# Gate rows and self-attention weights by way of DRAM, with a fuller set of fill work for the self-attention

## The reference

```python
c = jnp.cumsum(log_f, axis=1)
s = jnp.einsum('bqhd,bkhd->bhqk', qn, k) * scale
s = s + cqn[..., None] - c_keys          # c of the query minus c of the key
p = jax.nn.softmax(where(key <= query, s, -inf)); out = p @ v
```

```python
a = probs(q1, k1) - lam * probs(q2, k2)   # softmax with a relative bias, causal
o = a @ v                                  # head width 128
o = rms_norm(o, subln_g) * (1.0 - lambda_init)
y = multi_scale_pool(u, pool_w, pool_scale)
h = h + jnp.concatenate([o, y]) @ w_out
```

## Time and profile before

| what | value |
|---|---|
| runs, median of three | 2284.79 us |
| the profiled execution's own time | 2282.54 us |
| its span in the trace | 2280.8 us |
| DVE busy | 1280.7 us (56%) |
| ACT busy | 883.8 us (39%) |
| POOL busy | 13.9 us (1%) |
| PE's idle time in the whole span (span less PE busy) | 15.5 us |
| granted PE clock, mean | 0.998 |

### The profile page before, as it was taken

The page is one execution under the profiler, slowest core; times in us unless marked ns, Lnnn a source line. Parts: engine busy times, 40 slices in busy tenths (PEclk is TensorE's granted clock), DMA queues, the critical chain, the costliest instruction groups (busy, mean ns, idle before and its releaser), DMA issues.

```text
span 2280.8 us, 28255 instructions
## 1 busy us (share of the span) xinstructions
PE 2265.3 (99%) x11178; PEld 1844.8 (81%) x11178; DVE 1280.7 (56%) x2115; ACT 883.8 (39%) x1487; POOL 13.9 (1%) x14
## 2 busy tenths in 40 slices
PE   9999999999999999999999999999999999999998
PEld 7777778878777888788898888888888888888887
DVE  5865655567656556566555544444755536444445
ACT  5444533344445344364343422322322335332233
POOL 0000000000000000200000000000000000000000
PEclk9999999999999999999999999999999999999999
DMA  5655443336644334224353232223222213322231
GB/s 177 176 164 167 141 128 99 100 105 185 175 139 155 97 102 137 81 85 137 102 155 123 94 101 93 92 95 100 93 93 94 92 38 102 97 97 93 93 99 58
DMA packets 122471, 259.64 MB, mean 114 GB/s; under 512 B 12479, under 2 KB 66367, under 8 KB 122212
## 3 DMA queue, kind: packets, MB, share of 16 engines
q1 hardware_dynamic: 122340, 257.84, 36.2%
HBM read 229.73 MB, written 24.13 MB: 111 GB/s over the span
## 4 chain that ended last, share of the span: by engine, by line
PE 97%; DVE 1%; ACT 1%; POOL 0%; issue 0%; DMA 0%; SPq 0%; POOLq 0%; DVEq 0%; ACTq 0%
PE ps L378 28%; PE ps L380 27%; PE ps L379 27%; PE ps L621 2%; PE ps L729 2%; PE ps L404 2%; PE ps L405 2%; PE ps L406 2%; PE ps L1576 1%; PE ps L1515 1%; PE ps L470 1%; ACT t_Tb L190 1%; POOL t_UP L178 0%; PE ps L1013 0%; PE ps L1011 0%; PE ps L1012 0%
## 5 line engine op out<-in xcount | busy, mean ns | idle before, releaser
L378 PE MATMUL ps<-t_P0H,t_whi 128*128 128x512 f32 x1664 | 668.8, 402 | 1.7 <-DVE t_P0L L184 1.7
L380 PE MATMUL ps<-t_P0H,t_wlo 128*128 128x512 f32 x1664 | 656.3, 394 | 0.0
L379 PE MATMUL ps<-t_P0L,t_whi 128*128 128x512 f32 x1664 | 655.2, 394 | 0.0
L190 ACT ACTIVATE t_whi<-t_raw 128x1024 fp32r<-128x1024 f32 (+3 forms) x395 | 404.7, 1028 | 403.9 <-PE ps L380 330.1
L181 DVE TENSOR_TENSOR t_wlo<-t_raw,t_whi 128x1024 fp32r<-128x1024 f32 (+3 forms) x394 | 467.9, 1188 | 40.1 <-PE ps L406 19.9
L378 PEld LDWEIGHTS ps<-t_P0H,t_whi 128*128 128x128 f32 x1664 | 313.5, 188 | 95.5 <-issue 23.3
L380 PEld LDWEIGHTS ps<-t_P0H,t_wlo 128*128 128x128 f32 x1664 | 312.9, 188 | 72.8
L379 PEld LDWEIGHTS ps<-t_P0L,t_whi 128*128 128x128 f32 x1664 | 313.3, 188 | 71.4 <-issue 2.4
L378 PE MATMUL ps<-t_P1H,t_whi 128*128 128x512 f32 (+1 forms) x932 | 361.2, 388 | 0.3 <-DVE t_P1L L181 0.3
L379 PE MATMUL ps<-t_P1L,t_whi 128*128 128x512 f32 (+1 forms) x932 | 359.5, 386 | 0.0
L380 PE MATMUL ps<-t_P1H,t_wlo 128*128 128x512 f32 (+1 forms) x916 | 355.5, 388 | 0.0
(11 more groups left out here) (242 smaller groups left out, 2319.2 us busy)
## 6 DMA issues: line engine op xcount, KB each, us to landing
t_raw<-in_wts SPq DMA_DIRECT2D x362, 512.0 KB, 3.5
far<-t_Tb SPq DMA_DIRECT2D x26, 384.0 KB, 3.0
far<-t_Tb SPq DMA_DIRECT2D x16, 512.0 KB, 3.3
t_PTX<-far SPq DMA_DIRECT2D x64, 96.0 KB, 2.5
t_raw<-in_wts SPq DMA_DIRECT2D x16, 384.0 KB, 3.0
t_QKV<-far SPq DMA_DIRECT2D x32, 128.0 KB, 3.2
t_raw<-in_wts SPq DMA_DIRECT2D x13, 256.0 KB, 2.9
t_PTX<-far SPq DMA_DIRECT2D x24, 128.0 KB, 4.1
```

The lines of the kernel that those rows point to most:

```text
L190: return lambda e: e.activation(o, a, f, **k)
L378: e.matmul(bank[:, 0:N], wh, xh, start=first, stop=False)
L379: e.matmul(bank[:, 0:N], wh, xl, start=False, stop=False)
L380: return e.matmul(bank[:, 0:N], wl, xh, start=False, stop=end)
```

## The change

Four edits go together.

1. `forget()` turns the 128x16 running sums with one PE transpose, copies them to SBUF, writes them to a DRAM tensor `crow`, and reads them back with one DMA that repeats 2048 numbers on 128 partitions (1 MB). The four diagonals, spreads and copies go. The attention that follows starts after three fill steps (`lead=3`).
2. Stage E runs with `by_dma=True`. `norm` gets a branch for `nlam`: ACT scales map 1 in place, DVE adds map 2 in pieces of 128 and writes them in the layout for DRAM. One transfer carries both maps, 96 or 128 numbers per piece. PE's transposes and ACT's copies go; the freed PSUM bank joins the scores' and norms' banks.
3. Each head's norm runs by itself as soon as its values are done (`head_done`): four square roots of 4 columns, four spreads, between the units.
4. The second half of the values (`values_E(1)`) and the first half of output tiles 0 and 1 (the contraction steps of the pool's rows) become fill; tile 2 is begun after the last unit; then the three tiles take the heads' rows as they are ready. `prepare` runs on beside `project`.

```diff
+                if "nlam" in u:
+                    (t0, _), (t1, _) = u["T"]
+                    f4 = far[:, 0:128 * kh].rearrange("p (j k b) -> p k j b", j=4, b=32)
+                    z = [op(AC, act(t0[:, o1:o1 + n], t0[:, o1:o1 + n], ACT.Copy, scale=s[:, 12 + k:13 + k]), r)
+                         for k, (o1, n, _) in enumerate(parts)]
+                    r = op(DV, ts(s[:, 14:16], s[:, 14:16], u["nlam"], None, ALU.mult), r)
...
+                    o = [op(DV, stt(f4[:, b], cut3(t1, b), s[:, 14 + k:15 + k], cut3(t0, b), ALU.mult, ALU.add),
+                            z[k], r, ffree)
+                         for k, (o1, n, _) in enumerate(parts) for b in range(o1 // 128, (o1 + n) // 128)]
...
+            bank, free = SB.take()
+            p = op(PE, lambda e: e.transpose(bank[0:16, 0:128], byhead, ident[:, :]), o, free, c_I)
+            t, free = TMP.take()
+            a = op(AC, act(t[0:16, 0:128], bank[0:16, 0:128], ACT.Copy), p, free)
...
+            w = load(rows[0].rearrange("h (t p) -> (h t) p", p=128), t[0:16, 0:128], deps=[a])
...
+            w = load(CB.rearrange("p a b -> p (a b)"),
+                     rows.rearrange("a h n -> a (h n)").broadcast_to([128, 2048]), deps=[w])
             for h in range(4):
-                d = diagonal(cq.rearrange("p (t c) -> p c t", t=4)[:, h, :], o)
-                yield
-                ftok[h] = spread_it(d, dst=CB[:, h, :], B=SB)
+                ftok[h] = w
...
-                if n % 2:
+                if n in (1, 3, 5, 7, 9, 12):
                     next(steps, None)
...
+                  lead=3 if kind == "forget" else 0)
...
     def fill_E():
         yield from queries(1)
+        yield from values_E(1)
...
         yield from kv(0)
+        for m in range(2):
+            early.append(wo_E(m))
+            for _ in range(4):
+                next(early[m])
+                yield
...
+        def sums():
+            t, sq = got["sq"]
+            c = slice(136 + 4 * h, 140 + 4 * h)
+            r = stats(t, sq, out=lp[:, c], inv=1.0 / 128, B=SB)
+            TMP.give(t, r)
+            got["root"] = op(AC, act(lp[:, c], lp[:, c], ACT.Sqrt), r)
+            later(column)
...
-    drive(even_main(), fill_E(), 90, 42, lead=2)
+    drive(attention(eun, head_done, by_dma=True), fill_E(), 116, 30, lead=2)
+    early.append(wo_E(2))
+    for _ in range(4):
+        next(early[2])
+        flush()
+    for k in range(3):
+        assert P1.tok[k] is not None
+        for g in early:
+            next(g)
             flush()
```

More of the change, by code:

```diff
@@ L668, in norm, with cut3 @@
                 kh = u["cols"] // 128
+                if "nlam" in u:
[4 more added lines that the diff above has]
+                    r = op(DV, ts(s[:, 14:16], s[:, 14:16], u["nlam"], None, ALU.mult), r)
+                    def cut3(t, b):
+                        return t[:, 128 * b:128 * b + 128].rearrange("p (j b) -> p j b", j=4)
+                    o = [op(DV, stt(f4[:, b], cut3(t1, b), s[:, 14 + k:15 + k], cut3(t0, b), ALU.mult, ALU.add),
+                            z[k], r, ffree)
+                         for k, (o1, n, _) in enumerate(parts) for b in range(o1 // 128, (o1 + n) // 128)]
+                    TB.give(t0, o[-1])
+                    TB.give(t1, o[-1])
+                    STT.give(s, o[-1])
+                    u["far"], u["tiles"] = (far, o), kh
+                    return
                 f4 = far[:, 0:256 * kh].rearrange("p (j k b) -> p k j b", j=4, b=32)
@@ L732, in f @@
                 return i
-            p = op(PE, f, ready, u["vtok"], *[x[1] for x in held] if u["first"] else [])
+            p = op(PE, f, ready, u["vtok"]() if callable(u["vtok"]) else u["vtok"], *[x[1] for x in held] if u["first"] else [])
             if by_dma:
@@ L1127, in phase @@
             grouped.idle.append((wide(more), None))
-            drive(attention(units(kind, tk, npair, q, k, v), gate_y(slots, zslots, ztok), by_dma=True), fill, num, den)
+            drive(attention(units(kind, tk, npair, q, k, v), gate_y(slots, zslots, ztok), by_dma=True), fill, num, den,
+                  lead=3 if kind == "forget" else 0)
             grouped.idle = [x for x in grouped.idle if x[0].tensor.name == T["PTX"][:, :, :].tensor.name]
@@ L1297, in even_in, with values_E @@
             yield from gemm_fm(P0, w, parts8(), to_rows(1.0, kE[:, i, :], tok, ("k", i)))
[L1298 to L1301, removed]
+        yield from values_E(0)
+    def values_E(i):
+        yield from gemm_tm(P0, pair("ab_w_in", 0, 1024 + 256 * i),
+                           to_values([vE[:, :, 256 * i + 128 * d:256 * i + 128 * d + 128] for d in range(2)],
+                                     tok, [("v", 2 * i), ("v", 2 * i + 1)]))
     for i in range(2):
@@ L1308, in lay_out @@
         next(prep, None)
-    run(prep)
-    hrow, mcol, mrow, lamt = K["hrow"], K["mcol"], K["mrow"], K["lam"]
+    hrow = K["hrow"]
     def queries(i):
@@ L1376, in lay_out @@
         for n, _ in enumerate(project(g)):
+            next(prep, None)
             if n == 3 and g:
                 waiting.pop(g - 1)()
+    run(prep)
+    mcol, mrow, lamt = K["mcol"], K["mrow"], K["lam"]
     run(queries(0))
@@ L1424, in lay_out @@
                 bias=[BI4[h][:, 512 - n:512] for _, n, _ in parts], btok=btok[h], nlam=nlam,
-                vtok=[tok[("v", h)], lamt],
+                vtok=lambda h=h: [tok[("v", h)], lamt],
                 outs=[(0, 0, 128, [[vE[:, j, 128 * h:128 * h + 128] for j in range(n // 128)]
                                    for _, n, _ in parts], 0)]))
-    hs = {}
+    blocks.idle = [(UP[:, 0, 0:512], pooled[0])]
+    grouped.idle = [(UP[:, i, 0:512], pooled[0]) for i in (1, 2)]
+    turned.idle = list(PTS.idle)
+    SB.idle += PTP.idle
+    PTP.idle = []
     def head_done(u, banks, p):
@@ L1433, in head_done @@
         o = op(DV, lambda e: e.tensor_copy(qE[:, h, :], banks[0]), p)
+        got = {}
         def square():
[L1436 to L1442, removed]
+            got["sq"] = tmp_act_square(qE[:, h, :], o)
+            later(sums, 3)
+        def sums():
[5 more added lines that the diff above has]
+            later(column)
@@ new lines, in column, with row, scale @@
+        def column():
+            c = slice(152 + 4 * h, 156 + 4 * h)
+            r = op(DV, lambda e: e.reciprocal(lp[:, c], lp[:, 136 + 4 * h:140 + 4 * h]), got["root"])
+            got["diag"] = diagonal(lp[:, c], r)
+            later(row, 2 if h < 3 else 3)
+        def row():
+            got["row"] = spread_it(got["diag"], dst=kE[:, h, :], B=SB)
+            later(scale)
+        def scale():
+            q = op(DV, stt(qE[:, h, :], qE[:, h, :], lp[:, 134:135], kE[:, h, :], ALU.mult, ALU.mult), got["row"], lamt)
+            split_into(P1, h, qE[:, h, :], q)
@@ L1444, in head_done @@
         later(square)
         return [o]
-    def even_main():
-        yield from attention(eun, head_done, late_values=True)
-        for _ in range(4):
-            flush()
[L1451 to L1465, removed]
@@ L1467, in lay_out, with wo_E @@
-    drive(even_main(), fill_E(), 90, 42, lead=2)
-    drain()
+    xo = residual(1.0, lambda m, o: norm_tile(m, o, "xa0", P0, sqa), P0)
+    early = []
+    def wo_E(m):
+        w = Weight(chunk("ab_w_out", 0, halves(0), halves(128 * m, 1)))
+        return gemm_fm(P1, w, [(k, k) for k in (4, 5, 6, 7, 0, 1, 2, 3)], xo(m))
+    drive(attention(eun, head_done, by_dma=True), fill_E(), 116, 30, lead=2)
[7 more added lines that the diff above has]
+            next(g)
+            flush()
@@ L1470, in mixed @@
+    drain()
+    assert all(P1.tok)
+    for g in early:
+        run(g)
+    for m in range(3, 8):
+        run(gemm_fm(P1, Weight(chunk("ab_w_out", 0, halves(0), halves(128 * m, 1))), parts8(), xo(m)))
+    row_end()
     def mixed(name, i, rows, scale, gname, src):
@@ L1477, in mixed @@
             yield from gemm_fm(src, w, parts8(), ev(m))
-    run(mixed("ab_w_out", 0, halves(0), 1.0, "xa0", P1))
-    row_end()
     blocks.idle = [(E3[:, 9, :], None)]
     grouped.idle = [(E3[:, i, :], None) for i in (10, 11)]
-    turned.idle = [(ap, f) for ap, f in PTS.idle]
-    SB.idle += PTP.idle
-    PTP.idle = []
     def cross(l, gname):
@@ L1924, in build_program @@
         T["ps"] = ctx.enter_context(nc.psum_tensor("ps", [128, 8, 512], F32))
-        T["s_c"] = [sem(f"s_c{i}") for i in range(44)]
+        T["s_c"] = [sem(f"s_c{i}") for i in range(48)]
         T["s_w"] = [sem(f"s_w{i}") for i in range(NRAW)]
```

14 lines of the change are left out of this document (11 added, 3 removed).

## The result

The changed kernel takes 2271.12 us (median of 4 runs, 2269.93 to 2272.15), the kernel before 2283.93 beside it (2282.6 to 2285.78): 0.9944 of it, with 95% confidence 0.9931 to 0.9958, or 12.8 us less. The profiled execution took 2271.45 us, 11.1 less than that of before.

The account below looks back on a forecast made before the run. PE's issue was taken as the bound (busy 2265.3 of 2280.8 us). 17.4 us less and 2.4 more made 15.0 less than the profiled 2282.54: 2267.5, or 2268.5 with half the offset to the median; range 2261 to 2276.

Parts of the forecast that it names:

- Gate rows: Forget steps in two layers: eight spreads of 0.85 us go, one transpose per layer comes; net 6.3 us less.
- landing at 55.3: Gate rows' write and 1 MB repeated read: rows back at 55.3, or 58 if read half as fast; costed at nothing.
- Transposes and interruptions: Stage E: 40 PE transposes go, 3.2 us less, and 12 interruptions of the fill, 1.0 us less.
- Waits in stage E: PE's waits for DVE's map sums and ACT's copy go, with modelled ends and a slow stretch: 6.9 us less.
- 1.5 us for the clock: Stage E: the slow stretch after PE's longest wait goes, 3.35 us becoming 1.81; part of the waits' 6.9.
- What is late next: Stage E: map back about 14 us after its scores, values 21 us after; trip covered with 7 us to spare.
- DVE's limit: Stage E: turns and sums in pieces add 13 us to DVE, fill is denser; PE loses 1.5 us.
- rival 1: DVE with ACT becomes the bound in stage E's second half; PE loses 8 instead of 1.5: 2275 us; chance 0.14.
- Output tile 3: Fourth output tile: PE waits about 0.7 us for DVE to make its rest and empty the bank.
- tail's 0.2: Last head's norm comes within about 0.5 us of its 19 fill steps of cover; 0.2 us added.
- Rival 3: Everywhere: freed PE time returns as waits on DVE's weights; no change, 2282 to 2285 us; chance 0.06.
- rival 4: Stage E: DRAM trip exceeds three rounds, 21 us, in every unit; 3.5 us a unit, about 2310 us; chance 0.04.

Follow-up runs that it names:

- e1: Kernel before with only the gate rows' edit (new forget() steps, lead of 3); 2278.29 us, 0.9978 of before.
- e4: Changed kernel with PE transposing stage E's maps again instead of the trip through DRAM, fuller fill kept; 2274.11 us, 0.9962 of before.
- e3: Changed kernel with the values' second half made before stage E and output tiles begun only after its last unit; 2281.22 us, 0.9991 of before.
- e11: e3 with DVE's turn of unit i-2 queued behind the sums of unit i; 2276.08 us, 0.9968 of before.
- e5: Changed kernel with DVE's turn of unit i-2 in stage E queued behind the sums of unit i, not ahead; 2267.15 us, 0.9929 of before.
- e7: Changed kernel with stage E's values two rounds behind their scores instead of three; 2301.56 us, 1.0086 of before.
- e8: e5 with the mix's four products no longer in pairs: one ahead of a query projection, two between, one behind; 2272.61 us, 0.9955 of before.
- e10: Changed kernel with only the output tiles taken out of the fill and begun after stage E's last unit; 2271.87 us, 0.9951 of before.

## Why the prediction was right, and where it was not

The time came out 2.6 us above the forecast, inside the range and the likeliest case's bounds (near their upper end, 2272). Of the signs that I had named, PE's busy time (12.5 less), the clock of 1.00, the spreads and the wait on `t_X` came; "no line of stage E above 1 us" did not: there are two, of 1.3 and 1.5. In the sum itself, half of the offset of 2.25 us on 2267.5 is 2268.6, not 2268.5. By its steps, in the profiled executions (15.0 less foreseen, 11.1 found):

- **Gate rows, 6.3 less.** Size nearly right on PE (5.5 in e1 without the slow stretch, some 6 with the modelled ends of three new waits), time 4.8 (3.0 to 7.1 by the interval). The step that failed inside it is "three steps of 0.70 us of lead more" as a pure gain of cover: those steps are missing at the end, 2 x 0.44 us of waits, 1.2 with the modelled ends. The landing at 55.3 was right only as a sum: the small write and its follow-up took 3.4 us (50.87 - 47.49) where I had 2.4 from its issue on, the 1 MB read 4.45 (55.32 - 50.87) where I had 5.4.
- **Transposes and interruptions, 4.2 less.** e4 gives 3.0 by medians and 4.1 by the ratios (0.0018 of 2283), with 3.6 us in PE's busy time; its waits in stage E are 2.7 us (1.5 + 0.8 + 0.4) where the changed kernel's are 3.8, so by estimate the transposes and interruptions are worth about 4 (3.0 + 1.1). Right.
- **Waits in stage E, 6.9 less.** They went, and the clock is 1.00, but not for the reason I gave. I put them down to the trip and wrote that moving work into the fill "removes nothing from PE; it only fills rounds". e4 and e3 speak against it: without the trip PE still does not wait for the sums of maps, and without the fuller fill the other edits of stage E lose 2.9 us against e1 instead of winning (with the turn last they win 2.2, e11). That was the step that failed; the sum was saved, by luck, because both parts were in the change. The 1.5 us for the clock were luck too: they were in the trace that I read, but in e1 the same wait of 1.98 us costs none.
- **What is late next.** I asked only whether the values wait for the map, and found 7 us to spare. They do not wait, but DVE does, and what stands behind it. The first unit's scores started at 928.73, its map was turned at 945.52, its values came at 948.20: 2.7 us to spare. From scores to the start of the turn it is 16.2 us, where I had 14 (18.4 in the two units behind it, whose maps were back before DVE came to them); from scores to values 19.5, where I had 21. I had "one turn of at most 0.71 us on DVE" as busy time and forgot that a turn in an in-order queue is also a wait for a DMA, though the prediction asked just this of the gate rows.
- **DVE's limit, 1.5.** It measured 3.8 us of idle time (1.27 + 1.49 + 0.49 + 0.56), 4.4 with modelled ends of 0.16 each, and e5 gives back 4.0. Three of these four waits lay ahead of rival 1's place, the second half, and rival 1's cause was not theirs: in e5 DVE is 85% busy, every head still has its root between exponentials, and PE waits for nothing there. The rule of the Trainium skill ("ScalarE: Activation LUTs", section "Table sets: the hidden batching unit") thus decided nothing here: stage E has five table loads of 1.28 us in e5 and in the changed kernel where it had one, and in e5 they stay hidden.
- **Output tile 3, 0.7.** 0.54 us of idle time and 0.16 of modelled end: right. The tail's 0.2 did not come.

The sum closes: 15.0 less 2.9 (stage E, 4.4 for 1.5) less 1.2 (forget) plus 0.2 (tail) is 11.1, as found in these two executions. Rival 3 is out, since PE's 12.5 us show in the time; rival 4 is out, by 2.7 us. Its price for one wait (2.0 us and a slow stretch of 1.5) rested on one row; e7, which brings it about, costs 2.5 us a unit where I had 3.5.

## What to carry to other kernels

Before a step is queued on an in-order engine, ask not only how long it works but what it waits for and what stands behind it; here the place of the turn was worth 4 us, as much as a third of the whole change. When work moves off the bounding engine onto a longer path, the fill beside it is part of the price: here stage E's edits without the fuller fill lost 2.9 us (e3 against e1), and without the longer path won 4.2 (e4 against e1). e8 suggests, without a test of its own, that a product with a shared operand should not be spread out for the sake of banks before one has counted how long the operand then holds its buffer. And a slow stretch in one trace is not yet a price: look at the same stretch in a second trace of the same code before it goes into a sum.

## What was not expected of the hardware

- **Idling and the clock.** A wait of 1.98 us before stage E's transposes was followed by a slow stretch (clock 0.51), and I priced each wait of 2 us so. In e1 the same wait, of the same length, in the same code was followed by a clock of 1.00. In e10 one of 2.20 us and in e11 one of 1.97 us were followed by a clock of 1.00, in e8 one of 3.33 us by 0.51. So in these traces the length of one wait does not tell. The window behind it in e10:

```profile
954.00:956.00 2.00, 1.97 (x9) 1.62 (x10) 1.39 (x2) 2.00 (x4) 0.00 (x0) 1.00 0.80 223
```

- **Pieces of 384 bytes.** Writes of 192 KB in such pieces landed in 2.8 us, those of 256 KB in 512-byte pieces in 3.5; the reads in 2.0 and 2.1. The Trainium skill ("DMA: Bandwidth & Descriptors", section Specifications) has the engine read and modify before it writes below 512 bytes; no price of it is seen in these times.
- **The small write was no faster than a large one.** The gate rows' 8 KB took longer to land than the 192 KB of a map (same columns, 40 to 60 us; in the second layer 3.2 us for the 8 KB, 5.4 for the 1 MB):

```profile
t_M<-crow SPq DMA_DIRECT2D x1, 1024.0 KB, 4.2
crow<-t_TMP SPq DMA_DIRECT2D x1, 8.0 KB, 3.4
```
